# Slot gates of two experts in one product of 128 slots and two columns, taken by two copies of 64 partitions

## The reference, cut to what matters

```
gate_in = jnp.einsum('tk,tke->te', w_top, jax.nn.one_hot(e_top, E_PER_GROUP))
gate = g_onehot[:, :, None] * (p_top * gate_in)[:, None, :]
for gi in range(N_GROUPS):
    hid = silu(einsum('td,edf->tef', x, w_gate[gi])) * einsum('td,edf->tef', x, w_up[gi])
    y = y + einsum('tef,efd->td', hid * gate[:, gi, :, None], w_down[gi])
```

## Time and profile before

| | |
|---|---|
| three runs | median 1270.45 us (1268.3 to 1274.8) |
| the profiled execution | 1268.03 us |
| its span, first to last instruction | 1266.2 us |
| TensorE busy | 1136.2 us, 90% |
| VectorE, ScalarE busy | 494.3 us (39%), 321.2 us (25%) |
| mean granted clock of TensorE | 0.939 of full speed |

### The profile page before, as it was taken

One profiled execution on the slowest core, in us unless ns is written; L12 is line 12 of the kernel. 1 busy time (PEld: TensorE's weight loads), 2 busy tenths in 40 slices (PEclk: granted clock), 3 DMA queues, 4 the chain that ended last, 5 costly groups with the idle time before them and its releaser, 6 DMA issues.

```text
span 1266.2 us, 17985 instructions
## 1 busy us (share of the span) xinstructions
PE 1136.2 (90%) x7492; PEld 761.9 (60%) x7492; DVE 494.3 (39%) x1222; ACT 321.2 (25%) x608; POOL 45.2 (4%) x94
## 2 busy tenths in 40 slices
PE   3869999879697999999997899978897999999996
PEld 2669777667365555555544799645465455555544
DVE  0257443433525233333334433454425233333334
ACT  0166301122003111111112443454313111111114
POOL 0010000300001000000000200200001000000000
PEclk9579999979798999999999899999997999999998
DMA  9644221479483599999996344698680899999951
GB/s 282 200 134 134 67 75 59 132 245 343 161 331 133 205 412 382 368 376 367 372 360 214 102 150 151 224 330 306 229 324 18 325 409 383 362 364 376 373 197 43
DMA packets 122884, 317.18 MB, mean 250 GB/s; under 512 B 9136, under 2 KB 93136, under 8 KB 96166
## 3 DMA queue, kind: packets, MB, share of 16 engines
q1 hardware_dynamic: 115652, 304.87, 65.5%
q0 software_dynamic: 2336, 7.84, 1.9%
q10 hardware_dynamic: 4802, 3.18, 1.1%
HBM read 309.37 MB, written 6.49 MB: 249 GB/s over the span
## 4 chain that ended last, share of the span: by engine, by line
PE 80%; DVE 11%; ACT 3%; issue 2%; DMA 1%; SPq 1%; ACTq 0%; DVEq 0%
PE bank L1556 17%; PE bank L1127 11%; PE bank L1577 9%; PE bank L1519 5%; PE bank L1594 4%; PE bank L1190 4%; PE bank L1224 3%; PE bank L1091 3%; PE bank L1092 3%; PE bank L1093 3%; PE bank L1182 2%; DVE arena L2019 2%; DVE xT L2025 2%; PE bank L1086 2%; PE bank L1537 1%
## 5 line engine op out<-in xcount | busy, mean ns | idle before, releaser
L1556 PE MATMUL bank<-arena 128*64 128x512 f32 x768 | 225.2, 593 | 0.5 <-DVE gslot L2468 0.5
L1556 PEld LDWEIGHTS bank<-arena 128*64 128x64 f32 x768 | 71.7, 137 | 108.7 <-issue 108.0
L1715 ACT ACTIVATE arena<-bank 128x512 f32<-128x512 f32 (+7 forms) x159 | 78.6, 525 | 209.0 <-PE bank L1093 53.0
L1577 PE MATMUL bank<-ring,scratch 128*64 128x512 f32 x512 | 116.9, 599 | 1.1 <-ACT scratch L1715 1.1
L1556 PE MATMUL bank<-ring,arena 128*64 128x512 f32 x256 | 112.5, 592 | 0.0
L1091 PE MATMUL bank<-hTh,wh 128*128 128x320 f32 x304 | 96.2, 316 | 14.0 <-DVE wl L2084 14.0
L1127 PE MATMUL bank<-hT,ring 128*128 128x320 f32 x352 | 98.0, 435 | 0.6 <-issue 0.6
L1092 PE MATMUL bank<-hTl,wh 128*128 128x320 f32 x304 | 95.6, 314 | 0.0
L1093 PE MATMUL bank<-hTh,wl 128*128 128x320 f32 x304 | 95.5, 314 | 0.0
L2025 DVE SCALAR_TENSOR_TENSOR xT<-bank,mod,xT 128x256 f32<-128x256 f32 x144 | 69.1, 480 | 66.3 <-PE bank L1127 55.7
L2025 DVE SCALAR_TENSOR_TENSOR scratch<-scratch,gslot,bank 128x256 f32<-128x256 f32 x32 | 21.7, 678 | 163.3 <-ACT scratch L1935 163.3
(11 more groups left out here) (312 smaller groups left out, 1696.4 us busy)
## 6 DMA issues: line engine op xcount, KB each, us to landing
ring<-in_w_exp_down_dram SPq DMA_DIRECT2D x64, 1024.0 KB, 9.2
arena<-in_w_exp_gate_dram SPq DMA_DIRECT2D x48, 1024.0 KB, 8.8
arena<-in_w_exp_up_dram SPq DMA_DIRECT2D x48, 1024.0 KB, 11.3
ring<-in_w_ada_dram SPq DMA_DIRECT2D x44, 1024.0 KB, 9.7
ring<-in_w_exp_gate_dram SPq DMA_DIRECT2D x16, 1024.0 KB, 11.1
ring<-in_w_exp_up_dram SPq DMA_DIRECT2D x16, 1024.0 KB, 10.4
ring<-in_w_in_even_dram SPq DMA_DIRECT2D x14, 1024.0 KB, 5.4
ring<-in_w_qkv_odd_dram SPq DMA_DIRECT2D x8, 1024.0 KB, 5.4
```

The lines of the kernel that those rows point to most:

```text
L1556: ins = pe.matmul(bank[0][SLOTS * w:SLOTS * w + SLOTS, :].rearrange("p (w f) -> p w f", w=2), hg[:, q % 2, c, s0:s0 + SLOTS], weights[w][: ...
L1577: ins = pe.matmul(bank[2 + d][rows, :], hidT[:, P * f + SLOTS * w:P * f + SLOTS * w + SLOTS], x[:, w, D * f + 512 * d:D * f + 512 * d + 51 ...
L1715: return act.activation(dst, src, ACT.Copy)
```

## The change

The six pairs of products of a quad (two pairs of experts, three token tiles, two experts each) become six products: both experts of a pair at once, 128 slots as the stationary side and both experts' gate columns as the moving side. Each product so gives two columns, of which the slots of expert 0 need the first and the slots of expert 1 the second; the other two blocks are not used. Four columns of bank 0 are written in place of two. VectorE picks the right block with two copies, one for each half of the partitions, and raises `gate_taken` behind the second.

```
-                            for w in range(2):
-                                s0, e = P * h + SLOTS * w, 4 * q + 2 * h + w
-                                ins = pe.matmul(bank[0][SLOTS * w:SLOTS * w + SLOTS, 256 + h:257 + h],
-                                                perm[0:n, q % 2, t, s0:s0 + SLOTS].bitcast(F32), gates[0:n, t, e:e + 1],
-                                                start=(t == 0), stop=(t == 2))
+                            ins = pe.matmul(bank[0][:, 256 + 2 * h:258 + 2 * h],
+                                            perm[0:n, q % 2, t, P * h:P * h + P].bitcast(F32),
+                                            gates[0:n, t, 4 * q + 2 * h:4 * q + 2 * h + 2], start=(t == 0), stop=(t == 2))
...
-                    dve.tensor_copy(gslot[:, 2 * q:2 * q + 2], bank[0][:, 256:258]).then_inc(S["gate_taken"], 1)
+                    for w in range(2):
+                        rows = slice(SLOTS * w, SLOTS * w + SLOTS)
+                        ins = dve.tensor_copy(gslot[rows, 2 * q:2 * q + 2], bank[0][rows, 256 + w:260:2])
+                    ins.then_inc(S["gate_taken"], 1)
```

## The result

The changed kernel is slower: median 1284.67 us of 6 runs against 1269.05 us of 6 runs of the kernel before, a ratio of 1.0132 with an interval of 1.0099 to 1.0165. Measured again beside later experiments it was 1281.99 us against 1270.87 us, 1.0099 (1.0071 to 1.0126). The two intervals overlap; the medians lie 15.6 and 11.1 us apart, where the forecast was 9.7. The profiled execution took 1285.70 us, 17.7 more than the profiled one of before. What was L1537 is now L1535, and the lines behind it are two lower, up to the copies, which are L2468 as before; behind these, L2511 is now L2512.

What follows compares the result with a forecast made beforehand. TensorE was taken to bound the expert stretches. Longer slot gates in 14 quads, 8.7 us, plus quad 0 twice, 1.0 us, gave 9.7 us: 1279 us, range 1273.5 to 1285.

Steps and rivals of the forecast that it cites:

- what bounds the expert stretches: Both expert stretches: TensorE bounds them, busy 256.9 of 261 us and 262.7 of 267 us at full granted clock.
- pairs of narrow loads side by side: Slot gates: two experts' 64 column loads run together, 0.058 us a pair; 128 column loads take 0.113; +0.62 us a quad.
- no wait behind the step that would hide it: Down products behind the slot gates start without a wait, so 14 quads' 8.7 us all count.
- the copies covered: VectorE's copies in the other 14 quads cost nothing, under 4.48 us of idling; without that cover 1.3 us.
- rivals 1 to 3: Slot gates: passes set time, -8.6 us (4%); loads as fast as transposes', +0.1 us (5%); extra hidden, 1269 to 1272 (5%).
- the second copy: Quad 0 of either layer, where TensorE waits for the copy: a second one adds 0.09 us.
- The upper bound: Dearest load step: slot gates +0.72 us a quad, 0.16 for the second copy, 11.5 us, 1279.5 on the profiled run.
- the low bound: Cheapest load step: wide slot gate loads 0.06 us apart as in the transposes, +0.02 a quad, 0.1 us in all.
- rival 2: Slot gates: the wide load is as fast as in the transposes, 0.06 us apart; +0.1 us, 1268 to 1271; 5%.
- The clock falls: Expert stretches: longer narrow work halves the granted clock, 1.4 us a fall; three falls 13.8 us, 1284 on the median; 8%.

Runs made afterwards that it cites:

- b_full2: Kernel before with the slot gates and the transposes of perm over all 128 rows, nothing moved: 1257.82 us against 1269.02, ratio 0.9897.
- b_dense: Kernel before with four dense products ahead of each quad's slot gates: 1280.76 us against 1270.94, ratio 1.0100.

## Why the prediction was wrong

Right: what bounds the expert stretches; pairs of narrow loads side by side, twelve steps of 0.113 in place of twelve of 0.058 and four changes of shape, +0.62 us a quad, 1.70 predicted and 1.70 measured; no wait behind the step that would hide it; the copies covered; that rivals 1 to 3 do not hold.

Slightly off: the second copy, 0.17 us instead of 0.09, 0.16 us in all. The upper bound had 0.16 (its terms add up to 11.4, not 11.5).

Misread: the low bound and rival 2, the transposes' loads 0.06 apart. These two loads are the first behind a change of rows, 0.2 us after the load before them. Where transposes follow one another without a pause, their loads are 0.25 - 0.14 = 0.11 apart in the same trace, 0.6 us earlier, and (0.69 - 0.14) / 5 = 0.11 in b_full2, where all have 128 rows:

```profile
442.69 0.25 PEld L1584 LDWEIGHTS bank<-const,perm 128*128 128x128 f32 x2
...
444.35 0.69 PEld L1584 LDWEIGHTS bank<-const,perm 128*128 128x128 f32 x6
```

So the transposes keep the pace of the plain products, and the low bound of the load step rested on a pair that does not show the pace.

Wrong: the step "The clock falls". I gave it 8% and put nothing into the sum for it, because there was no fall in either expert stretch of the one profile and dense products stand on both sides. In both profiles of the changed kernel it happened, four and three times, 13.7 us at half clock in either: 6.8 of the 16.7 us in the first profile. That a stretch ran at full clock with 1.08 us of narrow work said nothing on 1.70 us of it. A fall of 3.4 us cost 1.7 us and not 1.4: of the 15 and 25 products of the earlier trace rows two each had started before the stretch, and their starts, 0.27 us apart at 0.50 and 0.15 at full clock, would have given 1.5. The price in the text, 13.8 us with three falls, lies between the two measured differences, 15.6 and 11.1, and beside the 14.0 of all runs; that is partly luck, for the first profile had four falls, at 1.7 each. What was wrong was the chance, and leaving the term out of the predicted time. How much of it a typical run pays is open: all runs together leave 4.1 us for it and all else.

Open: whether the narrow stretch or the longer quad brings the falls, why a fall comes behind one quad and not behind the next of the same length, and why the filler of b_dense, with two falls, did not do better than the kernel before.

## What to carry to other kernels

Where products have hardly any moving columns, count weight loads and what runs beside them, not instructions: two 64 column loads in the two halves of the array cost as much as one (0.058 us), and a 128 column load twice that. A change of rows or columns in the stationary shape costs 0.1 us each time here; filling a short tile up to 128 rows with zeros was worth 6 us. And price the clock with the step: when a change lengthens a stretch of narrow products, a half-clock stretch behind it belongs into the sum, counted in more than one profile and held against the mean of many runs. Moving such products between dense ones paid here by filling a wait, 0.2 to 0.4 us a quad; that it also keeps the clock up is not shown.

## What the hardware showed that was not expected

- Behind slot gates the granted clock went to 0.50 for 3.4 us at a time (once 6.8), from 1.1 to 3.4 us after the first of their loads, at 1.7 us for each 3.4, and in mostly different quads in two profiles of the same program. TensorE was busy throughout the stretches shown (3.41 of 3.41 us).
- Two small copies by VectorE out of one bank of PSUM, 64 partitions by 2 columns, stand 0.17 us apart, the second behind the end of the first; two others of similar size stand 0.09 apart and overlap. Ours begin at partitions 0 and 64, those both at partition 0, and they read 16 and 8 columns; no run tells which of these matters.
- A fast pair of loads can mislead: two loads of 128 columns of `perm` stand 0.06 us apart as the first two behind a change of rows, but 0.11 apart within a series of transposes (442.69 in the trace of before, 444.35 in b_full2), as for a plain product.
